# A two-block transformer kernel: memory keys in two halves, and another order of the first loads

## What is computed

```
# first block: two layers; m, mc = modulations of c and c_ctx
m  = silu(c)     @ ada_w[i] + ada_b[i]        # shift, scale, gate, shift, scale, gate
mc = silu(c_ctx) @ ada_w[i] + ada_b[i]
hn  = rms_norm(x, norm1_g) * (1 + scale) + shift
hcn = the same for the context ctx (256 tokens), with mc
layer 0: attention of hn over keys and values of hcn and hn, beside a gated
         31-tap convolution; h += gate * (... @ ev_w_out)
layer 1: short convolution mixer (sc_w_in, sc_w_out)
each layer then: h += gate * ec_moe(...)      # 16 experts, 32 tokens each, w_gate, w_up, w_down
# second block
h += parallel_mixer(...)                      # w_in_2, w_out_2
k, v = split(rms_norm(mem) @ xattn_wkv)       # mem: 256 tokens
k = rms_norm(k per head of 256)
h += attention(rms_norm(h) @ wq, k, v) @ wo
h += relu(rms_norm(h) @ w1)**2 @ w2
```

## Time and profile before

| | us |
|---|---|
| median of 3 runs | 1791.04 (1779.89 to 1792.28) |
| profiled execution, its device time | 1776.38 |
| its span | 1774.6 |
| PE busy / DVE / ACT / POOL | 1338.9 / 491.9 / 349.8 / 151.8 |
| moved by DMA | 561.76 MB, mean 317 GB/s |

### The profile page before, as it was taken

One profiled execution on the slowest core, in us unless ns is written; L12 is line 12 of the kernel. 1 busy time (PEld: TensorE's weight loads), 2 busy tenths in 40 slices (PEclk: granted clock), 3 DMA queues, 4 the chain that ended last, 5 costly groups with the idle time before them and its releaser, 6 DMA issues.

```text
span 1774.6 us, 18225 instructions
## 1 busy us (share of the span) xinstructions
PE 1338.9 (75%) x7746; PEld 778.3 (44%) x7746; DVE 491.9 (28%) x706; ACT 349.8 (20%) x515; POOL 151.8 (9%) x142
## 2 busy tenths in 40 slices
PE   4998866665686596579775655657557999899999
PEld 1753552121241141179521211212114867779997
DVE  1359450010110000056510100101004734446553
ACT  1111420000010000033300000000003633544442
POOL 1034000000000000010000000000003033440000
PEclk9999978788798798789887877877777978999999
DMA  9898839999979999994479999999999431434530
GB/s 346 359 383 347 325 134 396 422 422 422 414 322 422 413 417 419 414 365 183 154 315 422 422 422 422 422 421 422 422 422 353 175 111 53 160 120 177 184 114 24
DMA packets 109995, 561.76 MB, mean 317 GB/s; under 512 B 8516, under 2 KB 9908, under 8 KB 54126
## 3 DMA queue, kind: packets, MB, share of 16 engines
q1 hardware_dynamic: 106056, 551.83, 77.4%
q0 software_dynamic: 2208, 8.36, 1.2%
q10 hardware_dynamic: 1670, 0.68, 0.1%
HBM read 557.69 MB, written 3.16 MB: 316 GB/s over the span
## 4 chain that ended last, share of the span: by engine, by line
PE 39%; DMA 28%; DVE 3%; ACT 2%; issue 1%; SPq 1%; POOL 0%; DVEq 0%; ACTq 0%; POOLq 0%
PE ps L1841 23%; DMA ring<-in_moe_w_down 11%; DMA ring<-in_moe_w_up 10%; PE ps L2086 7%; DMA ring<-in_moe_w_gate 5%; PE ps L1826 3%; PE ps L2100 1%; SPq L472 1%; DMA ring<-in_w_in 1%; PE ps L2305 0%; PE ps L2293 0%; PE ps L2133 0%; PE ps L2295 0%; PE ps L1888 0%; PE ps L2383 0%
## 5 line engine op out<-in xcount | busy, mean ns | idle before, releaser
L2086 PE MATMUL ps<-ring,scratch 128*32 128x512 f32 x3072 | 478.6, 780 | 292.8 <-DMA ring<-in_moe_w_up 131.1
L2086 PEld LDWEIGHTS ps<-ring,scratch 128*32 128x32 f32 x3072 | 129.3, 138 | 616.5 <-issue 615.5
L1841 PE MATMUL ps<-ring_parts,scratch_parts 128*128 128x512 f32 x656 | 185.2, 401 | 5.1 <-DVE xT_parts L1156 1.4
L1841 PE MATMUL ps<-scratch_parts,ring_parts 128*128 128x256 f32 x704 | 146.0, 282 | 0.0
L1841 PEld LDWEIGHTS ps<-ring_parts,scratch_parts 128*128 128x128 f32 x656 | 122.3, 188 | 35.6 <-issue 4.9
L595 ACT ACTIVATE ring_parts<-ring 128x2048 fp32r<-128x2048 f32 x56 | 106.0, 1919 | 93.8 <-PE ps L1841 87.4
L1841 PEld LDWEIGHTS ps<-scratch_parts,ring_parts 128*128 128x128 f32 x704 | 116.2, 191 | 0.3
L438 DVE TENSOR_TENSOR ring_parts<-ring,ring_parts 128x2048 fp32r<-128x2048 f32 x44 | 100.7, 2289 | 53.4 <-ACT ring_parts L595 52.1
L1449 DVE TENSOR_TENSOR scratch<-ps,gate_bc 128x512 f32<-128x512 f32 x16 | 10.3, 686 | 299.7 <-PE ps L2086 299.7
L1441 DVE TENSOR_TENSOR scratch<-scratch,ps 128x1024 f32<-128x1024 f32 x8 | 9.8, 1222 | 292.0 <-PE ps L2086 292.0
L1841 PE MATMUL ps<-xT_parts,ring_parts 128*128 128x256 f32 x288 | 80.9, 281 | 1.3 <-DVE xT_parts L1147 1.3
(11 more groups left out here) (377 smaller groups left out, 1558.8 us busy)
## 6 DMA issues: line engine op xcount, KB each, us to landing
ring<-in_moe_w_gate SPq DMA_DIRECT2D x64, 2048.0 KB, 28.1
ring<-in_moe_w_up SPq DMA_DIRECT2D x64, 2048.0 KB, 27.3
ring<-in_moe_w_down SPq DMA_DIRECT2D x64, 2048.0 KB, 31.7
ring<-in_ada_w SPq DMA_DIRECT2D x24, 2048.0 KB, 12.2
ring<-in_mlp_w SPq DMA_DIRECT2D x16, 2048.0 KB, 8.5
ring<-in_sc_w_in SPq DMA_DIRECT2D x6, 2048.0 KB, 21.0
ring<-in_w_in SPq DMA_DIRECT2D x6, 2048.0 KB, 17.8
ring<-in_xattn_wkv SPq DMA_DIRECT2D x4, 2048.0 KB, 32.5
```

The lines of the kernel that those rows point to most:

```text
L1841: last = mm(out, lhs[x], rhs[y], start=start and n == 0, stop=stop and n == 2)
L2086: last = mm(ps[32 * j:32 * j + 32, banks[half], :], src[:, k, CAP * j:CAP * (j + 1)], w[j * RUN // EG][:, j % (EG // RUN), col:col + 512], ...
```

## The change

- The key stage is cut in two. `STREAM` has one chunk of `wk` after group 0, the other (`wk_rest`) after group 1, the values after group 2 as before; layer 0 has four loops of one group. The first half stage transposes and scales `mem`, multiplies with the first chunk and normalises into a tile of its own, `xk[0]`; PE waits for that normalisation before group 1. Its transposes and copies to `memkT` are done at the begin of the second half stage, then comes the second chunk with everything through to the store. The junk output of two squarings gets the name `mem_junk`.
- On SP the order is: modulation chunks 0 and 1, x, the wait and `ada_b`, chunk 2, the seven gains, chunk 3, `ev_q`, the context, `ev_kv` and on as before. c, c_ctx and the identity are issued by ACT at its begin. The other small loads are issued by ACT after it has scaled x (seven of them) and after the context (router weights and mask). The bias matmuls move from the last chunk to chunk 1.
- PE: `ada` 0, 1, 2, transposes of the gains, transposes of x, `ada` 3, its columns, then `ev_q` as soon as xT is there; then transposes of the context, `ev_kv` for x, `ev_kv` for the context, the filter's transposes, `ev_u`. DVE and ACT scale x before they touch the context. The context's transposes use PSUM banks 4 to 7 instead of 0 to 3.

```diff
-          ("ada0b_rest", 2), ... ("ev_out", 2), ("moe0", 48), ("wk", 2),
-          ("moe0b", 24), ("wv", 2), ("moe0c", 24),
+          ("ada0b_rest", 2), ... ("ev_out", 2), ("moe0", 24), ("wk", 1),
+          ("moe0b", 24), ("wk_rest", 1), ("moe0c", 24), ("wv", 2), ("moe0d", 24),
...
-        xk = at(0, t=NT, d=D)
+        xk = [at(8448, t=NT, d=512), at(0, t=NT, d=512)]
+        mem_junk = at(0, t=NT, d=D)
...
# SP
-            (c, c_ctx, ident, seven gains, wait cleared, ada_b)
-            modulations(0, (0, 1))
-            sp.dma_start(h, x)
-            modulations(0, (2, 3))
-            sp.dma_start(ctx_rows, ctx)
+            modulations(0, (0, 1))
+            sp.dma_start(h, x)
+            sp.wait_ge(sem("cleared"), 2)
+            sp.dma_start(ada_b[0:24, :], ada_b)
+            modulations(0, (2,))
+            (seven gains)
+            modulations(0, (3,))
             columns("ev_q", evw, 1)
+            sp.dma_start(ctx_rows, ctx)
             columns("ev_kv", evw, 1, width=256, col0=512)
...
-            columns("wk", a["xattn_wkv_2"], 2)
+            columns("wk", a["xattn_wkv_2"], 1)
             experts(LOOPS[1])
+            columns("wk_rest", a["xattn_wkv_2"], 1, col0=512)
+            experts(LOOPS[2])
             columns("wv", a["xattn_wkv_2"], 2, col0=D)
...
# ACT
-            (ten loads, params_in)
+            (c, c_ctx, ident: first_params_in)
...
             squares("x", h, xT_rows)
+            transposed("x", xT)
+            (seven loads, params_in)
             act.wait_ge(sem("ctx_in"), 16)
             squares("ctx", ctx_rows, by_token(flat(cT)))
-            transposed("x", xT)
             transposed("ctx", cT)
+            (router weights and mask: first_params_in)
...
# DVE
             normed("x", h, rows)
-            normed("ctx", ctx_rows, ctx_rows)
             ada_rows(0, 0)
             dve.wait_ge(sem("gain_cols"), 1)
             mod_cols(0, 0)
             transposed("x", xT)
+            normed("ctx", ctx_rows, ctx_rows)
             transposed("ctx", cT)
...
# PE, key stage
-            for j in range(2):
-                arrived(pe, FIRST["wk"] + j)
-                used(to_rows(FIRST["wk"] + j, memT, (4 + 2 * j, 5 + 2 * j)))
-            for j in range(2):
-                pe.wait_ge(sem("xk_normed"), j + 1)
-                row_transposes(xk, (4, 5, 6, 7), range(4 * j, 4 * j + 4))
+            used(to_rows(FIRST["wk"], memT, (4, 5)))
+            pe.wait_ge(sem("xk_normed"), 1)
+            experts(LOOPS[1])
+            key_transposes(0)
+            arrived(pe, FIRST["wk_rest"])
+            used(to_rows(FIRST["wk_rest"], memT, (6, 7)))
+            key_transposes(1)
             pe.wait_ge(sem("cols"), 4)
-            experts(LOOPS[1])
+            experts(LOOPS[2])
```

More of the change, by code:

```diff
@@ L733, in _ @@
             act.wait_ge(sem("mem_in"), 32)
-            act.wait_ge(sem("mo_h"), 4 * 2 + 1)
-            squares("mem", mem_rows, xk)
+            act.wait_ge(sem("mo_h"), 4 * 1 + 1)
+            squares("mem", mem_rows, mem_junk)
             act.wait_ge(sem("norm_T"), 4 * TRANSPOSED.index("mem") + 4)
@@ L747, in _ @@
                                              accum_out=sm[:, u:u + 1]).then_inc(sem("xk_ss"), 1)
-            for b in (1, 3):
-                act.wait_ge(sem("cols_ps"), b + 1)
-                nc.scalar.activation(flat(memkT[:, 2 * b:2 * b + 2, :]), pb(4 + b), ACT.Copy).then_inc(sem("cols"), 1)
-            experts(LOOPS[1])
+                if j:
+                    key_columns(1)
+                experts(LOOPS[1 + j])
             u = NORMS.index("mem")
@@ L1793, in ada @@
                             (ident[:, r:r + 1].broadcast_to([P, 32]), ada_b)
-                        last = mm(ps[32 * j:32 * j + 32, bank, :], lhs, rhs, start=(c == k == 0), stop=(k == 2))
+                        last = mm(ps[32 * j:32 * j + 32, bank, :], lhs, rhs, start=(c == k == 0), stop=(c == 3 and k == 1))
                 used(last)
@@ L1910, in _, with kv_rows @@
             pe.wait_ge(sem("mod_cols"), 1)
+            normed_columns("x")
+            i = FIRST["ev_q"]
+            arrived(pe, i)
+            used(to_rows(i, xT, (0, 1)))
+            def kv_rows(bank, lhs):
+                i = FIRST["ev_kv"]
+                for t in range(NT):
+                    for k in range(KD):
+                        last = mm(ps[:, bank, 256 * t:256 * t + 256], lhs[:, k, P * t:P * (t + 1)], slot8(i)[:, k, 0:256],
+                                  start=(k == 0), stop=(k == KD - 1))
+                return last
             transposes("ctx", ctx_rows)
-            normed_columns("x")
+            arrived(pe, FIRST["ev_kv"])
+            kv_rows(2, xT)
             normed_columns("ctx")
+            used(kv_rows(3, cT))
             pe.wait_ge(sem("params_in"), PARAMS * 16)
@@ L1918, in _ @@
             last.then_inc(sem("cw_ps"), 1)
-            i = FIRST["ev_q"]
-            arrived(pe, i)
-            used(to_rows(i, xT, (0, 1)))
-            i = FIRST["ev_kv"]
-            arrived(pe, i)
-            for bank, lhs in ((2, xT), (3, cT)):
-                for t in range(NT):
-                    for k in range(KD):
-                        last = mm(ps[:, bank, 256 * t:256 * t + 256], lhs[:, k, P * t:P * (t + 1)], slot8(i)[:, k, 0:256],
-                                  start=(k == 0), stop=(k == KD - 1))
-            used(last)
             pe.wait_ge(sem("cw"), 1)
@@ L2142, in _, with key_transposes @@
             normed_columns("mem")
-            for j in range(2):
-                arrived(pe, FIRST["wk"] + j)
-                used(to_rows(FIRST["wk"] + j, memT, (4 + 2 * j, 5 + 2 * j)))
-            for j in range(2):
+            def key_transposes(j):
                 pe.wait_ge(sem("xk_normed"), j + 1)
-                row_transposes(xk, (4, 5, 6, 7), range(4 * j, 4 * j + 4))
+                for k in range(4):
+                    for t in range(NT):
+                        last = nc.tensor.transpose(pb(4 + 2 * j + k // 2)[:, N * (k % 2) + P * t:N * (k % 2) + P * (t + 1)],
+                                                   xk[j][:, t, P * k:P * (k + 1)], ident)
+                    if k % 2:
+                        last.then_inc(sem("cols_ps"), 1)
+            i = FIRST["wk"]
+            arrived(pe, i)
+            used(to_rows(i, memT, (4, 5)))
+            pe.wait_ge(sem("xk_normed"), 1)
+            experts(LOOPS[1])
+            key_transposes(0)
+            i = FIRST["wk_rest"]
+            arrived(pe, i)
+            used(to_rows(i, memT, (6, 7)))
+            key_transposes(1)
             pe.wait_ge(sem("cols"), 4)
-            experts(LOOPS[1])
+            experts(LOOPS[2])
             for j in range(2):
```

100 lines of the change are left out of this document (54 added, 46 removed).

## The result

The changed kernel takes 1761.81 us (median of 4 runs, 1754.62 to 1776.27) beside 1790.19 us for the kernel before (4 runs, 1779.89 to 1792.28): ratio 0.988, 95% interval 0.983 to 0.993. The prediction was 1773.0, or 0.990. The profiled run took 1768.46 us, its span is 1766.7; the profiled run of before had 1774.6. So the two profiles differ by 7.9 us only, and the two medians by 28. Neither is the worth of the change, and where the difference between them comes from is half of what follows.

What follows compares the result with a forecast made beforehand. Before the experts the computation chain sets the pace, in expert stages the weight stream. Key stage -10 and start -8 give -18 us: 1776.4 to 1758.4, plus 14.7 to the median, 1773.0 (0.990); range 1760 to 1786.

Steps and rivals of the forecast that it cites:

- Key stage, -10: Memory key stage: halving it removes nearly all of 10.5 us of DMA standstill; -10 us, bounds -10.5 to about -7.
- The chunk model: Key halves: the stream runs dry nine chunks of 4.97 us, 44.7 us, after a group's last pair starts.
- Rival 2: Key halves still run dry, release 2 to 4 us late: -3 to -7 there, time 1778; chance 0.12.
- Rival 3: Key stage split pays fixed steps twice, PE sets the pace: +7 us in sum, time 1798; chance 0.04.
- Start, -8 at ev_u: Start: earlier loads and new order begin ev_u at 65.8 instead of 74.35, 8.5 us earlier, taken as -8.
- ada_b's wait: Start: PE waits for ada_b behind x before its first modulation matmul; early arrival would win less than 1 us.
- Rival 1: Start gains only 2.5 to 5 us, from low clock or late loads; time 1777; chance 0.20 with milder form.
- its milder form: Start: only the fourth chunk runs slowly, behind the transposes; sum -16.3, time 1775; within the joint chance of 0.20.
- Rival 4: Start's reordering does nothing, as a wait before the experts is stream-bound: -10 alone, time 1781; chance 0.04.
- The shift passes: From ev_u to the experts: the start's gain carries through unchanged, and the stream carries it on.
- The step from the span to the median: Whole time: 14.7 us between the earlier kernel's profiled run and its median, added to 1758.4 to give 1773.0.
- rival 5: Whole time: more than 20 us won through a clock staying high or early ada_b; 1769 or less; chance 0.05.

Runs made afterwards that it cites:

- e12: The changed kernel unedited, timed a third time in the same rounds as the version with eight extra float32 matmuls; ratio 0.991 to the kernel before.
- e1: The kernel before with only the key stage cut in two halves, its old start kept; ratio 0.994 to the kernel before.
- e2: The kernel before with only the new start, its key stage left whole; ratio 0.995 to the kernel before.
- e6: The changed kernel with the first key half's 32 matmuls done twice, to overrun its margin on purpose; ratio 0.996 to the kernel before.
- e5: The changed kernel with ada_b issued on ACT's queue behind the identity instead of SP's behind x; ratio 0.991 to the kernel before.
- e8: The changed kernel with loads in the old order, computation on PE, DVE and ACT in the new order; ratio 0.995 to the kernel before.

## Why the prediction was right, step by step

**The time and its sum.** Forecast -18 us, ratio 0.990; measured 0.988, 0.992 and 0.991, that is -14 to -22 on 1790. At the points of the trace where the change can be read alone it is -20.1 (end of layer 0), from parts of -10.0 and -10.1. The three medians, 1761.8, 1768.2 and 1768.0, all lie below the 1771.5 to 1775 that I gave the forecast for itself, so the ratio was met and the time was put too high; the last paragraph of this section says why. With the late stage equal, the profile of e12 has a span of 1755.9 and that of before 1774.6: -18.7. The lowest groups of run times say the same: before 1774.6 to 1778.5 (on the chip of e12), e1 1764.6 to 1769.4, e2 1765.1 to 1768, after 1754.6 to 1757.7, some 10 us for each part and 20 for both.

**Key stage, -10.** Right in mechanism and size: -10.0 (e1: -9.1). The chunk model, 44.7 us from the start of the last pair, gives 384.9 and 510.9; SP issued again at 382.70 and 508.72, 2.2 us in time in both halves where 1.3 and 0.8 were reckoned. Even so the first lost 1.0 us and the second nothing (0.6 together expected): a margin of 2 us is not quite free of loss, and why one half pays and the other doesn't no run tells. In e6 the count of nine chunks failed: it holds only where the wkv slot is released before the other eight are spent. The detour's parts were 14.00 and 13.90 for the matmuls and 5.71 and 5.50 of idle time behind them, against 14.0 and 5.4. Rival 2 is out by its size, since it wanted 3 to 7 us lost and 1.0 was; but its sign, a stretch below 400 GB/s behind a half stage, did appear, at 395 in the first half here and at 376 (1.7 us) in e1. The second half and the value stage have 424 and 415. In e6 another 14 us in the half cost 16.7. Rival 3 is out by PE's waits of 4.25 and 4.67 us for the chunk ahead of each half.

**Start, -8 at ev_u.** 66.34 for 65.8, so 8.0 for 8.5, and -8 was the term. Step by step: first modulation matmul 17.07 (17.6), held as forecast; second and third chunk without a pause, done at 25.0 (26.1); fourth at 1.92, done at 30.3 (31.5); copy to end of xT 3.83 (3.85, where the two times named give 3.83); ev_q 34.53 (35.4). What was gained there ev_q gave back, 15.49 long instead of 14.00, its first matmuls at the lower clock behind 2.71 us of idle time; I had put it at 14.0. The gap to ev_u was 31.8 (30.4). DVE's copy of the conv weights held PE for 0.39 (0.35), and the small loads on ACT's queue show in no wait of PE up to there. That ada_b's wait is harmless, as forecast (less than 1 us), is shown by e5. Rival 1 and its milder form failed on 1.92 for the fourth chunk and on ev_q at 34.53; in e8, with the old loads, the fourth chunk does begin slowly, at 3.10. Rival 4 is out by e2.

**Where the term was mis-sized.** "The shift passes" was right in sign, but it grew: 8.0 us at ev_u are 10.1 at the first gather (e2: 7.5 and 9.5). Two things make most of it. The rows, two of before and then the same two places in after:

```profile
206.26 1.04 PE L1794 MATMUL ps<-scratch,cst 128*32 128x512 f32 x8
...
242.22 7.01 PE L2051 MATMUL ps<-router_w,xT 128*128 128x16 f32 x32 [1.23 <-ACT xT L580]
```

```profile
187.15 1.04 PE L1808 MATMUL ps<-scratch,cst 128*32 128x512 f32 x8
...
233.86 5.48 PE L2070 MATMUL ps<-router_w,xT 128*128 128x16 f32 x32 [1.40 <-ACT xT L572]
```

The bias matmuls moved from the last chunk to chunk 1 in every group of modulations and not at the start alone. In the last group they stood behind the last chunk on PE's path in before; in after they lie in a wait for ACT, which is 2.13 us instead of 2.99. That is 0.9 us which my sum had left out. And the router's matmuls took 5.48 us instead of 7.01, 1.5 us, since the clock was full for a larger part of them. Against these go some 0.3 us in small pieces. The second gain isn't bound to the change: the router's matmuls took 5.15 us in e1 with the old start, and 7.01 in e6 with the new one. Nor is the rest of the stretch steady. From ev_u to the first gather it took 183.2 to 183.3 us in nine of the profiles with the new start, and 188.7 in e6; there the window from 140 to 160 has a granted clock of 0.77, where after has 1.00. With e6 in place of after, only 4.0 us would have been left of the start's gain at the first gather. I had passed a shift through a stretch whose clock differs from run to run of the same code.

**The step from the span to the median** is the weak one. I put the 14.7 us between before's profiled run and its median on the forecast as if it were noise of measurement. By the groups above it is the distance between runs with a short and with a long late stage, and the profile I read happened to be of the short kind; a long one of the kernel before was never profiled, so this is inferred. The forecast of 1773 stands 5 to 11 us above the measured medians for that reason and for the 2 us above. All three medians lie where I had put rival 5 (1769 or less), with a clock that stays high or an early ada_b as its reasons; neither is seen in the start. The parts measured give 20.1, and what took the first median down to 1761.81 is mainly which groups the four runs fell in. That the first ratio, 0.988, came so near to 0.990 is in part luck for the same reason.

## What to carry to other kernels

Where a stream of weights feeds a ring, a detour of computation is free as long as the slots last; count the slots that really come free inside it, and split a detour that is longer so that each piece stays under that count, with more than 2 us to spare: 2.2 us were enough in one place here and lost 1.0 us in another. Early loads and the order of their consumers may have to be changed together: each alone was worth nothing here, and together they gave 8 us at ev_u. A shift that is won early can grow or shrink in a stretch whose clock is not steady, so its worth at the end is read from more than one profile. Before trusting a difference of under 1%, compare the length of each untouched stage in both profiles; if one comes in two lengths, compare profiles of the same length, or the milestones before it.

## What the hardware showed that I had not expected

The granted clock can fork. With the same instructions, the same durations up to that point and a fall at the same place, it came back after about 31 us or after about 61, and the second case cost 13.4 us of 1770, in one stage of small float32 matmuls and transposes in which PE looks busy (20.00 of 20 us). The rows at 0.50 are the only sign; the busy share shows nothing. Eight float32 matmuls of 512 columns ended it, in two profiles of two; four did not hold (0.76, then 0.50), and six more at the place where it falls made it 13 us longer. The two lengths are measured; what chooses between them is open.
